# Reading the moving operand's columns in turn from both halves of its row, in the weight chunks of two feed-forward layers and two query projections

## The reference, cut to what matters

```
# memory_cross_attention
q = (h @ w_q)                                   # 256x1024 @ 1024x1024
# swiglu, F = 2816
(silu(h @ w_gate) * (h @ w_up)) @ w_down        # 1024x2816 twice, then 2816x1024
```

## Time and profile before

| | before |
|---|---|
| median of 2 runs | 1122.75 us (1121.3 to 1124.2) |
| the profiled execution's own time | 1121.39 us |
| its span | 1120.1 us |
| TensorE busy | 1088.6 us, 97% of the span |
| VectorE, ScalarE, GpSimd busy | 748.8, 582.9, 49.2 us |
| mean granted clock of TensorE | 0.999 |

### The profile page before, as it was taken

One profiled execution on the slowest core, in us unless ns is written; L12 is line 12 of the kernel. 1 busy time (PEld: TensorE's weight loads), 2 busy tenths in 40 slices (PEclk: granted clock), 3 DMA queues, 4 the chain that ended last, 5 costly groups with the idle time before them and its releaser, 6 DMA issues.

```text
span 1120.1 us, 15289 instructions
## 1 busy us (share of the span) xinstructions
PE 1088.6 (97%) x6205; PEld 944.3 (84%) x6205; DVE 748.8 (67%) x1023; ACT 582.9 (52%) x938; POOL 49.2 (4%) x82
## 2 busy tenths in 40 slices
PE   3999999999999999999999999999999999999997
PEld 3689988788888988988988988788988989888986
DVE  4637676865788978546687854556967545788743
ACT  2347654444458766655434444556664546444442
POOL 3021000000010000000000000000011000000000
PEclk9999999999999999999999999999999999999999
DMA  9965354755646324534655556544444436555450
GB/s 343 339 196 168 132 188 134 275 193 169 213 145 192 114 63 163 187 114 136 178 186 183 188 207 200 179 166 151 151 151 165 139 113 205 188 188 188 155 184 37
DMA packets 118358, 195.08 MB, mean 174 GB/s; under 512 B 6297, under 2 KB 39217, under 8 KB 118288
## 3 DMA queue, kind: packets, MB, share of 16 engines
q1 hardware_dynamic: 115728, 187.51, 49.9%
q0 software_dynamic: 2560, 6.60, 2.1%
HBM read 193.04 MB, written 1.05 MB: 173 GB/s over the span
## 4 chain that ended last, share of the span: by engine, by line
PE 83%; DVE 10%; ACT 4%; DMA 1%; issue 1%; POOL 1%; SPq 0%; ACTq 0%; DVEq 0%; POOLq 0%
PE product L666 55%; PE product L703 5%; PE small L703 5%; DVE conv_out L2683 4%; PE small L705 3%; PE product L705 3%; PE product L968 2%; ACT w_high L590 1%; DVE w_low L600 1%; PE small L813 1%; PE small L2045 1%; DMA w_raw<-in_w_ada 1%; PE small L728 1%; PE small L1415 1%; ACT diagonal L2576 1%
## 5 line engine op out<-in xcount | busy, mean ns | idle before, releaser
L600 DVE TENSOR_TENSOR w_low<-w_raw,w_high 128x2048 fp32r<-128x2048 f32 (+3 forms) x160 | 349.9, 2189 | 178.1 <-ACT w_high L590 173.8
L590 ACT ACTIVATE w_high<-w_raw 128x2048 fp32r<-128x2048 f32 (+3 forms) x160 | 292.1, 1831 | 176.8 <-PE product L666 145.5
L666 PE MATMUL product<-w_high,H 128*128 128x512 f32 (+2 forms) x736 | 239.5, 393 | 0.1
L666 PEld LDWEIGHTS product<-w_high,H 128*128 128x128 f32 x736 | 137.9, 188 | 28.4 <-issue 2.2
L666 PE MATMUL product<-H,w_high 128*128 128x256 f32 x816 | 150.4, 282 | 0.2 <-ACT queries_keys L1062 0.2
L666 PE MATMUL product<-w_low,H 128*128 128x512 f32 (+2 forms) x368 | 142.3, 387 | 0.0
L666 PEld LDWEIGHTS product<-H,w_high 128*128 128x128 f32 x816 | 126.6, 188 | 2.2 <-issue 1.3
L666 PE MATMUL product<-H,w_low 128*128 128x256 f32 x408 | 114.3, 280 | 0.0
L703 PE MATMUL product<-H,w_high 128*128 128x512 f32 x256 | 89.1, 391 | 0.0
L703 PE MATMUL small<-H,w_high 128*128 128x512 f32 x256 | 89.1, 391 | 0.0
L666 PEld LDWEIGHTS product<-w_low,H 128*128 128x128 f32 x368 | 69.3, 188 | 11.7 <-issue 0.2
(11 more groups left out here) (402 smaller groups left out, 1761.2 us busy)
## 6 DMA issues: line engine op xcount, KB each, us to landing
w_raw<-in_ffn_w_gate SPq DMA_DIRECT2D x20, 1024.0 KB, 5.0
w_raw<-in_ffn_w_up SPq DMA_DIRECT2D x20, 1024.0 KB, 5.0
w_raw<-in_ffn_w_down SPq DMA_DIRECT2D x20, 1024.0 KB, 4.9
w_raw<-in_w_merge SPq DMA_DIRECT2D x16, 1024.0 KB, 5.0
w_raw<-in_w_ada SPq DMA_DIRECT2D x16, 512.0 KB, 8.8
w_raw<-in_mem_w_k SPq DMA_DIRECT2D x8, 1024.0 KB, 4.9
w_raw<-in_mem_w_v SPq DMA_DIRECT2D x8, 1024.0 KB, 4.9
w_raw<-in_conv_w_pw SPq DMA_DIRECT2D x16, 512.0 KB, 4.8
```

The costliest lines, as they stand in the source:

```text
L590: k.act.eng.activation(parts_of(k, i, j)[0], raw_of(k, i), ACT.Copy).then_inc(*k.act.tells("weights_high", ("weights high", i)))
L600: k.vec.eng.tensor_tensor(low, raw, high.bitcast(F32), ALU.subtract).then_inc(*k.vec.tells("weights_low", ("weights low", i)))
L666: mm = pe.eng.matmul(bank[:, off:off + wide], a, r, start=b not in started, stop=True, skip_group_check=True)
```

## The change

64 chunks get an entry of their own in `places`: where in its slot the high part lies, where the low part lies, and a group width. Where the width is not zero, `dealt` changes the order in which the columns of each matmul stream: the row is taken as two halves, and groups of `width` columns come in turn from the first half and from the second. The output columns are written in the same order, so that each lands where it did. For the 2x256 matmuls of L703 the two halves are the high and the low part of `H`, which lie 8192 bytes apart; within a row of 512 weights they lie 1024 bytes apart, within 256 tokens 512 bytes. Nothing is computed that was not computed before.

All slots of `w_high` get room for 32 numbers instead of 8, taken out of the small room ahead of them, and begin 128 bytes before a line; the default places are moved so that chunks without an entry lie as before relative to a line. `w_first`, which shares the space of `w_high` in the first stage, moves by 96 bytes against a line, and a room for statistics shrinks by 8 numbers, which moves what follows it by 32 bytes, up to the next operand that is laid on a line.

The entries are:

- `w_down`, 24 chunks: width 8 in 5, 2 in 3, 16 in 5, 4 in 4, 32 in 3, 64 in 2, 128 in 2; the high part 128 bytes before a line, or 32, 64, 96 or 128 bytes further; the low part 64 or 32 bytes before a line or on it
- `mem_w_q_2`, 8 chunks: width 8 in 5, 4 in 1, 16 in 2
- gate and up of kind "apart", 32 chunks: width 8 in 20, 16 in 4, 4 in 4; 4 keep the old place and order (entry `(24, 4, 0)`).

```diff
-HIGH_ROOM, LOW_ROOM = 8, 16
-HIGH_AT = {"turned": 8, "still": 0, "apart": 0}
+HIGH_ROOM, LOW_ROOM = 32, 16
+HIGH_AT = {"turned": 32, "still": 24, "apart": 24}
 LOW_AT = {"turned": 16, "still": 8, "apart": 4}
...
-        self.room(432)
+        self.room(424)
...
+def place(k, i):
+    return k.places.get(i, (HIGH_AT[k.plan[i][2][0]], LOW_AT[k.plan[i][2][0]], 0))
+
+def dealt(x, width):
+    return x.rearrange("p (h a b) -> p a h b", h=2, b=width) if width else x
+
+def explored(plan):
+    def of(name, kind):
+        return [i for i, (pieces, _, into) in enumerate(plan) if into[0] == kind and name in pieces[0][0].tensor.name and sum(n for _, n in pieces) == CN]
+    places = {}
+    down = of("ffn_w_down", "turned")
+    for i, (width, high, low) in zip(down, [(8, 8 * d, 16) for d in range(5)] + [(2, 16 * d, 16) for d in range(3)] + [(16, 8 * d, 8) for d in range(5)] + [
+            (4, 8 * d, 0) for d in (0, 2, 3, 4)] + [(32, 16 * d, 16) for d in range(3)] + [(64, 0, 0), (64, 32, 0), (128, 0, 0), (128, 32, 0)]):
+        places[i] = high, low, width
+    for i, (width, high) in zip(of("mem_w_q", "still"), [(8, 8 * d) for d in range(5)] + [(4, 0), (16, 0), (16, 32)]):
+        places[i] = high, 8, width
+    for n, i in enumerate(of("ffn_w_", "apart")):
+        places[i] = [(24, 4, 0), (24, 8, 8), (0, 0, 8), (8, 16, 8), (16, 4, 8), (32, 0, 8), (24, 4, 16), (0, 0, 16), (24, 4, 4), (0, 0, 4)][n // 2 % 10]
+    return places
...
-                    mm = pe.eng.matmul(bank[:, off:off + wide], a, r, start=b not in started, stop=True, skip_group_check=True)
+                    mm = pe.eng.matmul(dealt(bank[:, off:off + wide], width), a, dealt(r, width), start=b not in started, stop=True, skip_group_check=True)
...
-                pe.eng.matmul(bank[:, :].rearrange("p (i n) -> p i n", n=S), high[:, j, column], x.parts[:, :, first + j, :], start=first + j == 0,
-                              stop=True, skip_group_check=True)
-                mm = pe.eng.matmul(bank[:, 0:S], low[:, j, column], x.high[:, first + j, :], start=False, stop=True, skip_group_check=True)
+                parts = x.parts[:, :, first + j, :]
+                both = (bank[:, :].rearrange("p (i n) -> p i n", n=S), parts) if not width else (
+                    bank[:, :].rearrange("p (i a b) -> p a i b", i=2, b=width), parts.rearrange("p i (a b) -> p a i b", b=width))
+                pe.eng.matmul(both[0], high[:, j, column], both[1], start=first + j == 0, stop=True, skip_group_check=True)
+                mm = pe.eng.matmul(dealt(bank[:, 0:S], width), low[:, j, column], dealt(x.high[:, first + j, :], width), start=False, stop=True,
+                                   skip_group_check=True)
```

More of the change, by code:

```diff
@@ L296, in __init__ @@
         self.plan = weight_plan(w)
+        self.places = explored(self.plan)
         self.split = [i for i, (_, _, into) in enumerate(self.plan) if into[0] in HIGH_AT or into[0] == "whole"]
@@ L573, in parts_of @@
 def parts_of(k, i, j):
-    kind = k.plan[i][2][0]
-    return [chunk_view(k, t[j][:, at[kind]:], i) for t, at in ((k.w_high, HIGH_AT), (k.w_low, LOW_AT))]
+    high, low, _ = place(k, i)
+    return [chunk_view(k, t[j][:, at:], i) for t, at in ((k.w_high, high), (k.w_low, low))]
+def place(k, i):
[15 more added lines that the diff above has]
+    return places
 def chunk_view(k, t, i):
@@ L653, in pe_block @@
         high, low = parts_of(k, k.split[i], i % k.N_SPLIT)
+        width = place(k, k.split[i])[2]
         pe.wait_ge(("weights low", k.split[i]), x.ready(first // CK))
```

## The result

The changed kernel took 1145.51 us (median of 2 runs, 1145.0 to 1146.03) against 1122.75 us: 1.0212 times the time before, 95% interval 1.0186 to 1.0238. It is slower by 23 us; whether by more than 2% two runs leave open. Its profiled execution took 1146.03 us with a span of 1144.7, so 24.6 us of span are to be found.

The account below looks back on a forecast made before the run. TensorE's matmul time was taken to bound the kernel. A third of matmuls at good distances (-6.4 us) and two thirds at bad (+4.5 us) gave -1.9 us: 1119.5 profiled, 1121 us as median; range 1103 to 1163.

Parts of the forecast that it names:

- TensorE's time per matmul is the kernel's time: Whole kernel: TensorE busy 1088.6 of 1120.1 us, so each nanosecond per changed matmul counts and nothing else lies on the path.
- the bookkeeping of slots and of `w_first`: Wider slots and moved `w_first`: claimed free; were `w_first` to lose 10.8 ns in each of 96 matmuls, 1.0 us.
- what the change does to it: Changed matmuls' reads: small groups let moving and weight reads go in step, distance deciding; value taken together -1.9 us.
- the contiguous price of a bad place: All 1808 changed matmuls at a bad place in a contiguous stream: 3.7 ns each, +6.7 us, 1128.1 us.
- the forecast's own case: Changed matmuls partly in step, a third at a good distance, two thirds at a bad one: 1119.5 us, chance 0.50.
- rival 3: Moving stream of changed chunks: each of 96.4 thousand jumps costs a 0.417 ns cycle, 40.2 us, 1161.6 us; chance 0.15.
- The last sentence of the prediction: Changed chunks: wrong if jumps cost anything steady, or two reads in step collide at each group, making 3.7 ns no bound.
- threshold of 0.24 ns a jump: Jumps in changed chunks: from 0.24 ns each, 23 us in 96.4 thousand, the kernel is slower by over 2%.
- Rival 4: Changed fp32r columns, reading or writing PSUM: broken-up stream falls to half rate, +297 us, 1418 us; chance 0.05.
- Rival 2: Changed matmuls: loss is a fixed price per fp32r weight load, address pattern free, 1121.4 us; chance 0.28.

## Why the prediction was wrong

The forecast was 1121 us and no change; the kernel became slower by 2.1%. The range, 1103 to 1163, held the time.

- *Right:* TensorE's time per matmul is the kernel's time: the parts' sums from starts gave 1134.6 and 1139.4 us for kernels that took 1134.6 and 1139.06 (that the first fits to the tenth is luck: the kernel before took 1120.75 us beside it, where I had put 1121.2). Nothing else lies on the path; the bookkeeping of slots and of `w_first` costs nothing.
- *The step that failed* is the value taken for "what the change does to it": that a small group lets the moving read go in step with the weight read, so that a third of the matmuls lose their loss and the others pay at most 3.7 ns, together -1.9 us. The runs showed +24.6 us, all of it in the read, with no dependence on the distance that this mechanism is about (242.5 to 243.4 ns at five places). The observation under it, that the place matters, was right for the contiguous stream (3.9 us, up to 8 ns a matmul), and wrongly carried over to the grouped one. What sets the price of the dealt read is open beyond the reading of the last section.
- *The bound:* I took the contiguous price of a bad place, 3.7 ns, as the upper end of the forecast's own case, though rival 3 stood beside it with the right side and the right order, at 0.15. The last sentence of the prediction names the way in which it went wrong. The chance was too small: a stream that no row of the trace shows deserved more than one in five for a steady cost.
- *Rival 3, one cycle a jump,* gave 1161.6 us. It has the shape only roughly: 106 ns at width 2 as it said (107), but 25 and not 53 at width 4, 16.5 and not 26 at width 8, 14 and not 13 at width 16, and nothing at 64 and 128 at a good place. Its threshold of 0.24 ns a jump was just passed by the mean, 24.6 us in 96.4 thousand, 0.26 ns. But the price isn't one per jump: taking 15.3 thousand jumps out gave back 6.1 us by the starts, where one price of 0.24 ns gives 3.6.
- *Rival 4, half rate,* is right for what didn't stand in the change: skipped groups of 2, and groups of 4 off a multiple of 16, at 452 and up to 446 ns. In PSUM it is wrong at all widths tried: the write side took what the place takes. Of the two sentences on PSUM on the page "Advanced Engine Details and Errata" (Memory Cachelines) of the Trainium skill, the runs bear out the second (two consecutive elements are enough) and not the first.
- *Rival 2, nothing,* had the place as free, and places alone cost 3.9 us. The page "TensorE: Matmul & The Clock Gate" (Part 2) of the Trainium skill says that loading weights takes no read bandwidth from the running matmul. The trace agrees insofar as the dealt loss doesn't hang on the distance between the two reads; but the run with `hidden` moved, 233.1 ns against 226.7, shows that the loaded operand's place is not without effect.

## What to carry to other kernels

For an fp32r matmul's moving operand, keep innermost runs at four float32 numbers or more that begin on a multiple of 16 bytes, and begin the whole row on a 256-byte line (up to 8 ns a matmul here). A run broken every 8 bytes cost 50 to 116% of the stream, and the one such pattern tried in plain float32 5%. Runs of 16 bytes or more cost between -1 and +23%, with the step between them, so a grouping is to be measured at its own step. Where a matmul's output goes in PSUM, by runs of two columns or more, was free at all widths tried, so that a permutation wanted in the result belongs on the write side. Before a cost is bounded by the nearest row, ask whether the row's resource is at its limit there: a loss of 5% against the ideal in every matmul was a hint that it might be.

## What the runs showed that I had not expected

- The matmul's read seems to come in aligned pieces of 16 bytes, at 1.68 to 1.77 ns each in the plainer cases (table above, with the cases that don't fit).
- The same 128 breaks of a row cost between -3 and +51 ns with the step alone: 224 ns at 64 bytes, 278 at 256. The 256-column matmuls order the steps in the same way.
- Reading groups of four columns at steps of 64 bytes made the whole kernel 0.3% faster, though not in `w_down`.
- A stream of like matmuls can settle at one of two speeds at the same place, by what ran before it: 229 or 234 ns in row order, 223 or 227 ns at steps of 64 bytes.
